# Meta rows of two projection pairs: fp32 products of four raw weight tiles in four 32-column tiles

## What is computed

```
meta = meta_tokens[None]                 # 16 rows
h = concatenate([meta, x1], axis=1)      # 16 + 512 rows, 2048 wide
hn = rmsnorm(h, attn_norm_w)
proj = hn @ w_in                         # a_k and a_v are columns 1024 to 3071
```

## Time and profile before

| | |
|---|---|
| median of three runs | 1591.24 us (1591.22 to 1592.08) |
| profiled execution | 1591.43 us, its span 1589.6 us |
| PE (matmul) | busy 99% of the span |
| DVE, ACT, POOL | 56%, 51%, 42% |
| granted TensorE clock, mean | 0.998 |

### The profile page before, as it was taken

How to read it: one execution, slowest core, us unless ns; L and a number is a source line. 1 busy time by engine, 2 the same in 40 slices (tenths; PEclk the granted TensorE clock), 3 DMA queues, 4 the chain that set the end, 5 groups by cost and what they waited for, 6 DMA issues and landing times.

```text
span 1589.6 us, 21772 instructions
## 1 busy us (share of the span) xinstructions
PE 1578.3 (99%) x8015; PEld 1301.0 (82%) x8015; DVE 887.9 (56%) x1843; ACT 812.2 (51%) x1692; POOL 674.9 (42%) x569
## 2 busy tenths in 40 slices
PE   9999999999999999999999999999999999999998
PEld 7788888888888888898787788888888888888886
DVE  4257657674357776468554441423355454876675
ACT  5456766764334455444344356444466664344561
POOL 5553434436766304675110035544444326664022
PEclk9999999999999999999999999999999999999999
DMA  9454655656888978858998847654554325625762
GB/s 346 127 177 97 155 125 158 160 119 144 195 204 187 240 242 264 233 177 187 258 254 284 210 155 273 191 140 140 160 156 128 102 79 140 152 80 152 245 239 106
DMA packets 139382, 285.39 MB, mean 180 GB/s; under 512 B 11227, under 2 KB 17820, under 8 KB 138604
## 3 DMA queue, kind: packets, MB, share of 16 engines
q1 hardware_dynamic: 85660, 164.49, 31.3%
q0 software_dynamic: 31664, 81.70, 25.1%
q10 hardware_dynamic: 21952, 37.81, 7.3%
HBM read 259.01 MB, written 92.06 MB: 221 GB/s over the span
## 4 chain that ended last, share of the span: by engine, by line
PE 98%; issue 1%; DVE 0%; ACT 0%; POOL 0%; DMA 0%; POOLq 0%; ACTq 0%; DVEq 0%
PE acc L718 15%; PE acc L720 15%; PE acc L719 15%; PE acc L734 4%; PE acc L736 4%; PE acc L735 4%; PE turn L1194 3%; PE acc L888 2%; PE acc L886 2%; PE acc L887 2%; PE sc L886 2%; PE sc L887 2%; PE turn L886 2%; PE turn L887 2%; PE sc L888 2%; PE turn L888 2%
## 5 line engine op out<-in xcount | busy, mean ns | idle before, releaser
L1939 POOL TENSOR_TENSOR w_lo<-w_raw,w_hi 128x512 fp32r<-128x512 f32 x341 | 509.5, 1503 | 654.3 <-ACT w_hi L1317 653.3
L1317 ACT ACTIVATE w_hi<-w_raw 128x512 fp32r<-128x512 f32 x565 | 354.2, 629 | 454.3 <-PE acc L720 182.4
L718 PE MATMUL acc<-w_hi,setA_hi 128*128 128x512 f32 (+1 forms) x820 | 330.5, 403 | 0.5 <-ACT stage L1331 0.4
L720 PE MATMUL acc<-w_hi,setA_lo 128*128 128x512 f32 (+1 forms) x820 | 315.8, 385 | 0.0
L719 PE MATMUL acc<-w_lo,setA_hi 128*128 128x512 f32 (+1 forms) x820 | 314.8, 384 | 0.0
L2364 DVE TENSOR_TENSOR w_lo<-w_raw,w_hi 128x512 fp32r<-128x512 f32 x224 | 154.6, 696 | 139.3 <-ACT w_hi L1317 138.7
L720 PEld LDWEIGHTS acc<-w_hi,setA_lo 128*128 128x128 f32 x820 | 153.9, 188 | 31.6
L718 PEld LDWEIGHTS acc<-w_hi,setA_hi 128*128 128x128 f32 x820 | 154.4, 188 | 26.2 <-issue 2.1
L719 PEld LDWEIGHTS acc<-w_lo,setA_hi 128*128 128x128 f32 x820 | 154.7, 189 | 24.0
L734 PE MATMUL acc<-setA_hi,w_hi 128*128 128x512 f32 x256 | 101.9, 398 | 0.0
L736 PE MATMUL acc<-setA_lo,w_hi 128*128 128x512 f32 x256 | 99.9, 390 | 0.0
(11 more groups left out here) (555 smaller groups left out, 3251.2 us busy)
## 6 DMA issues: line engine op xcount, KB each, us to landing
w_raw<-in_swa_w_in SPq DMA_DIRECT2D x35, 1024.0 KB, 7.3
w_raw<-in_w_in SPq DMA_DIRECT2D x32, 1024.0 KB, 5.2
w_raw<-sum_out SPq DMA_DIRECT2D x64, 256.0 KB, 4.6
sum_k<-in_w_in POOLq DMA_DIRECT2D x24, 512.0 KB, 6.5
sum_out<-in_swa_w_out POOLq DMA_DIRECT2D x24, 512.0 KB, 7.9
sum_v<-in_w_in POOLq DMA_DIRECT2D x24, 512.0 KB, 7.9
w_raw<-in_w_in SPq DMA_DIRECT2D x48, 256.0 KB, 5.5
sum_out<-in_w_out POOLq DMA_DIRECT2D x24, 512.0 KB, 6.5
```

Source lines behind the costliest of these rows:

```text
L718: mm(acc[t][:, 0:cols], hi[:, kc, rows], wh, start=(k == 0), stop=False)
L720: last = mm(acc[t][:, 0:cols], lo[:, kc, rows], wh, start=False, stop=(k == K - 1))
L1317: nc.scalar.activation(w_at(f)[0], raw_of(f), ACT.Copy).then_inc(done, 1)
L1939: nc.gpsimd.tensor_tensor(lo, raw_of(f), hi.bitcast(F32), ALU.subtract).then_inc(s_lo, 1)
```

## The change

The meta rows of the two pairs are no longer made from `w_hi` and `w_lo` but from `w_raw`, in plain fp32, with the meta tokens unsplit in a new tile `meta_full` (41 units of 16 columns: zeros, the tokens, their negatives). The stationary operand has 32 columns (16 rows for chunk a, 16 for chunk b), so that a product fills a quarter of the array's columns. Four pieces that belong to two successive values T of the pair's row index are taken together: piece n of the four writes partitions 32n to 32n+31 of `acc[2]`. The call `meta_products(c, M)`, M = 0 to 7, first waits for the landing of its four raw tiles, which are pieces 6M, 6M+1, 6M+3, 6M+4 in the first half (M < 4) and 6M, 6M+2, 6M+3, 6M+5 in the second. It stands after row block 0 of piece 1 for M = 0 and of piece 6M-1 for the others. `meta_product` and its 128 matmuls go; 16 calls of four fp32 matmuls come.

Since PE now reads `w_raw`, `free_tile` gains a second wait: the place of such a piece is free only when `s_used` shows that the piece at which `meta_products` stands has been done. The sum of four quarters instead of two parts takes DVE three additions instead of one; ACT's copy is as it was, of one quarter. The windows of `project_meta`, which stays, shrink from 96 to 80 columns. ACT fills `meta_full` with one activation more; DVE clears it once and makes two subtractions less.

```diff
-FULL = 96
+FULL = 80
@@ free_tile
                 eng.wait_ge(s_wlo, number[f - 8] + 1)
+            if f - 8 in meta_use:
+                eng.wait_ge(s_used, meta_use[f - 8])
@@
+        def meta_tiles(c, T):
+
+            if T < 8:
+                unit = SIGNED_AT + 3 * H1[c][T]
+                return (3 * T, unit + 1), (3 * T + 1, unit)
+            unit = 2 * (H2[c][T - 8] - 8)
+            return (3 * T, unit + 1), (3 * T + 2, unit)
+
+        meta_use = {}
+        for c in ("k", "v"):
+            for T in range(16):
+                for p, _ in meta_tiles(c, T):
+                    meta_use[B[c] + p] = B[c] + max(6 * (T // 2) - 1, 1) + 1 + 4
+
+        def meta_quarter(bank, n):
+
+            return bank[2 * META * n:2 * META * (n + 1)]
@@ PE
-            def meta_product(c, p, unit, start, stop):
-
-                wh, wl = w_at(B[c] + p)
-                mm(acc[2][0:FULL, :], meta_window(unit), wh, start=start, stop=False)
-                last = mm(acc[2][0:FULL, :], meta_window(unit), wl, start=False, stop=stop)
-                if stop:
+            def meta_products(c, M):
+
+                of = (*meta_tiles(c, 2 * M), *meta_tiles(c, 2 * M + 1))
+                for p, _ in of:
+                    slot, i, target = raw_at[B[c] + p]
+                    pe.wait_ge(s_tile[4 * slot + i], target)
+                for n, (p, unit) in enumerate(of):
+                    last = mm(meta_quarter(acc[2], n), meta_full[:, unit:unit + 2].rearrange("p a b -> p (a b)"),
+                              raw_of(B[c] + p), start=(M == 0), stop=(M == 7))
+                if M == 7:
                     last.then_inc(s_meta, 1)
@@ ACT
-                        nc.scalar.activation(metaT[:, SIGNED_AT + n:SIGNED_AT + 32:4], meta_f[:, 0:8], ACT.Copy, scale=sign)
+                        nc.scalar.activation(meta_full[:, SIGNED_AT + 1 + n:SIGNED_AT + 24:3], meta_f[:, 0:8], ACT.Copy, scale=sign)
+                    nc.scalar.activation(meta_full[:, 1:16:2], meta_f[:, 8:16], ACT.Copy)
@@ DVE
+                if m in (1, 2):
+                    for n in (0, 2):
+                        after(dve, V.tensor_tensor(total, meta_quarter(bank, n), total, ALU.add))
+                    V.tensor_tensor(total, meta_quarter(bank, 3), total, ALU.add).then_inc(s_mevac, 1)
+                    return
```

More of the change, by code:

```diff
@@ L70 @@
     SUM_SLOT[of] = slot
-SIGNED_AT, META_UNITS = 4 * KC + 1, 104
+SIGNED_AT, META_UNITS, FULL_UNITS = 16, 4 * KC + 2, 41
 HALF = S // 2
@@ L243, in build @@
         metaT = sb("metaT", [P, META_UNITS, META], F32R)
+        meta_full = sb("meta_full", [P, FULL_UNITS, META])
         alibi_h = over("alibi_h", [P, 2, ALIBI_AT[NT]], MASK)
@@ L1005, in project_mid @@
                                 product(c, p, i, setA_hi[:, h1[m], top], setA_lo[:, h1[m], top], X0[i], m == 0, m == 7)
[L1006 to L1011, removed]
                             elif j == 1:
@@ L1018, in project_mid @@
                                 product(c, p, i, mx_hi[:, 0, m, top], mx_lo[:, 0, m, top], acc[i][:], m == 0, m == 7)
-                                if i == 0:
-                                    meta_product(c, p, 4 * h1[m], False, False)
+                                if i == 0 and m == 0:
+                                    if c == "k":
+                                        pe.wait_ge(s_evac, 4 * E[14] + 4 + 3)
+                                    else:
+                                        pe.wait_ge(s_mevac, 3)
+                                    meta_products(c, 0)
                             else:
@@ L1026, in project_mid @@
                                 product(c, p, i, mx_hi[:, 1, m, top], mx_lo[:, 1, m, top], X1[i], m == 0, m == 7)
+                                if i == 0 and m % 2 == 1:
+                                    meta_products(c, m // 2 + 1)
                 for m in range(8):
@@ L1036, in project_mid @@
                                 product(c, p, i, setA_hi[:, h2[m], top], setA_lo[:, h2[m], top], X0[i], m == 0, m == 7)
-                                if i == 0:
-                                    meta_product(c, p, 4 * h2[m] + 1, False, False)
                             elif j == 1:
@@ L1046, in project_mid @@
                                 product(c, p, i, my_hi[:, 1, m, top], my_lo[:, 1, m, top], acc[i][:], m == 0, m == 7)
-                                if i == 0:
-                                    meta_product(c, p, 4 * h2[m], False, m == 7)
+                                if i == 0 and m in (1, 3, 5):
+                                    meta_products(c, m // 2 + 5)
                 for m in range(8):
@@ L2479, in _ @@
                         V.memset(metaT[:].bitcast(F32), 0.0)
+                        V.memset(meta_full[:], 0.0)
                 if m == 3:
@@ L2509, in _ @@
             dve.wait_ge(s_metaH, 1)
-            top_hi = metaT[:, 1:4 * 8:4].bitcast(F32)
-            V.tensor_tensor(metaT[:, SIGNED_AT + 2:SIGNED_AT + 32:4], meta_f[:, 0:8], top_hi, ALU.subtract)
-            V.tensor_tensor(metaT[:, SIGNED_AT + 3:SIGNED_AT + 32:4], top_hi, meta_f[:, 0:8], ALU.subtract)
             V.tensor_tensor(metaT[:, 3:4 * KC:4], meta_f[:], metaT[:, 1:4 * KC:4].bitcast(F32), ALU.subtract).then_inc(s_metaT, 1)
```

## The result

| | before | after |
|---|---|---|
| median of the runs | 1591.23 us (1590.13 to 1592.08) | 1603.34 us (1602.58 to 1604.01) |
| ratio | | 1.0075 (95% interval 1.0063 to 1.0087) |
| profiled execution, its span | 1591.43, 1589.6 us | 1604.01, 1602.2 us |
| up to the key pair's first product | 745.6 us | 747.8 us |
| key pair | 92.0 us | 103.6 us |

The kernel became 12.1 us slower; 5.9 us faster was predicted. The stages are read between starts of `product`'s first matmul on PE's timeline. In the profiled execution they differ by +2.2, +11.6, -2.1 and +0.9 us: nearly all of the loss is in the key pair. (Of the 2.2 us, 1.6 are waits of PE for POOL's low parts near 508 us in this one execution.

The account below looks back on a forecast made before the run. PE, busy 99% of the span, was taken to bound the kernel. Groups against removed matmuls gave -10.5 us, new waits +4.6, in sum -5.9: from 1591.43 to 1585.5 us, range 1580.2 to 1597.3.

Parts of the forecast that it names:

- The lower of the two bounds: On PE, the 16 new groups cost 19.7 us if four tiles run side by side; the other bound was 60.8.
- rows 5 and 6: Profile rows before, line 851 on PE: two fp32 column tiles start together and run fully side by side.
- The small edits: DVE's further sums, ACT's copy, meta_full's clearing and narrower project_meta windows: covered or too small to show, 0 us.
- Rival 1: In the pairs, loads are never late: -10.5 us, 1580.7 us; chance 0.08.
- The strict-order rival (4): On PE, matmuls start in strict order, a group takes five rounds, 2.5 us, 16 take 40.2: 1604 us; chance 0.06.
- Rival 3: On PE, moving operands can't be read for four tiles at once, a group costs 2.1 us: 1597.2 us; chance 0.14.
- the new waits: PE's waits for raw tiles needed earlier, in both pairs: 4.6 us, between nothing and 6.6.
- Landings of before against the time at which the group would stand: Late-tile estimate from the earlier trace: key pair M=2 and M=6, value pair M=5, 2.8 us in all.
- I cost it at nothing: SP's load of piece 6M+8, delayed about 3.5 us by free_tile's added wait: mostly covered before ACT wants it, 0 us.
- The bound of 6.6: Upper bound of PE's waiting: the key pair gives back all its gain, 5.3 us, and the value pair 1.3.
- Rival 2: Key pair bound by its loads, SP's later issues adding: over 7.3 us of stall, within 0.2% of before; chance 0.12.
- The sign that would show it wrong: PE's waits over 7 us or on low parts, or a group not near 1.2 us.

Follow-up runs that it names:

- experiment 1: Changed kernel, but its groups multiply resident token tiles instead of raw weight tiles, without landing waits or free_tile's added wait: 1579.86 us, ratio 0.9928.
- experiment 2: Changed kernel, its groups multiplying resident token tiles without landing waits, but with free_tile's added wait kept: 1579.32 us, ratio 0.9926.
- experiment 3: Changed kernel, its groups multiplying resident token tiles, with the landing waits kept but free_tile's added wait gone: 1590.34 us, ratio 0.9994.
- experiment 7: Changed kernel with groups M=1 to 7 one piece later (6M) and their places held as much longer: 1593.76 us, ratio 1.0025.
- experiment 8: Changed kernel with groups M=1 to 7 two pieces later (6M+1) and their places held as much longer: 1593.06 us, ratio 1.001.
- experiment 10: Changed kernel with groups M=1 to 7 one piece later (6M) and the first group one piece earlier (piece 0): 1594.12 us, ratio 1.0014.
- experiment 9: Changed kernel, but each pair's first group multiplies a resident token tile, with no landing wait or held places for it: 1597.74 us, ratio 1.0044.
- experiment 5: Changed kernel with most of POOL's block sums moved out of the pairs, one quarter staying at the key pair's start: 1598.51 us, ratio 1.0045.
- experiment 4: Changed kernel with 32 groups of two raw tiles instead of 16 of four, at piece 3T-1: 1599.45 us, ratio 1.0049.
- experiment 11: Change in the value pair alone; the key pair has the matmuls of the kernel before, on stand-in windows: 1592.51 us, ratio 1.001.
- experiment 12: Change in the value pair alone, its groups M=1 to 7 two pieces later; key pair with the earlier matmuls on stand-ins: 1589.39 us, ratio 0.9989.

## Why the prediction was wrong

**Right.** The groups alone are -11.3 us by experiment 1 (forecast -10.5), and a group costs 1.20 us (forecast 1.23). The lower of the two bounds, chosen by the form of rows 5 and 6, was the true one. The small edits cost nothing that experiments 1 and 2 would show. Rival 1 had the right worth for groups that never wait: 1580.7 against the 1579.86 of experiment 1.

The strict-order rival (4) gave 1604 us, within 1 us of what was measured, and that is a coincidence: it had 40.2 us for the groups and 2.8 of waits, where the traces have about 19 and 16.8. By mechanism it is out. The Trainium skill, "TensorE: Matmul & The Clock Gate", section on packing small matmuls, says that matmuls start in program order and that a weight load runs beside a matmul in flight only if the row groups differ. All tiles here are 128 rows deep, so their row groups are the same. Yet four start within 0.03 us, and a group of four costs as much as a group of two (1.20 and 1.18): the trace doesn't agree with the rule as it was applied to this case. Rival 3, the moving operands as a limit, is out by the same numbers.

**Wrong: the new waits.** The step that failed is the term "the new waits" of the sum: 4.6 us with an upper bound of 6.6. The trace has 16.8 us of waiting, and 4.7 us more that come of it. Three parts of the term failed.

1. "Landings of before against the time at which the group would stand" gave three late groups, and the trace of the need alone (experiment 3) has three, one at a place that was named for the key pair (M=2) and one for the value pair (M=5), 5.3 us in all. The kind was right, and so was the reading: the trace of before has these three and no others. But the landings were those of a single execution. In that same trace the last tile of three more groups lands only 0.2 to 0.5 us ahead of the need (M=5 and M=7 of the key pair, M=6 of the value pair). Ten executions give times over a range of 9 us, and their median puts the need at 10.5 us. The bound of 6.6 rested on that one execution too.

2. "I cost it at nothing", of SP's held loads. The reason given looked at when ACT wants piece 6M+8. Against that consumer it is right, and experiment 2 shows it: nothing. But the change brings a second, earlier consumer of the same loads, the group M+1, six pieces behind group M, and only four for M=0. The load that the hold delays and the tile that the next group wants early are the same: piece 10 is issued 4.8 us later and wanted 3.8 us after its issue, where the tiles that PE waits for in after take 5 to 8 us to land. Each edit was priced against the kernel before, none against the other. The square of experiments gives -0.5, +10.5 and, together, +23.5: the step that cost nothing is worth 13 us. In the traces of experiments 1 and 2 the hold takes the last tile's time from issue to need from 8.9 to 3.8 us at M=1 of the key pair and from 8.5 to 6.5 and 6.1 at M=2 and 3. In the second half that time is the same with and without it (6.0, 4.3, 5.9 and 6.0 against 5.9, 4.3, 5.7 and 6.0 us): there only the tiles ahead of the last go out later, and the late landings of M=5 and 7 in after aren't the last tile's later issue. What the hold adds there isn't separated from the early need. Moving the groups within the ring of eight places (experiments 7, 8 and 10) brings M=1 to five or six pieces behind the first group, but no group to more than six: it gains 9 to 10 us of the 23.5.

3. What a wait does to the clock wasn't in the sum. Against experiment 1 the key pair of after is 103.6 - 86.0 = 17.6 us longer: 12.9 are the waits, 4.7 the matmuls behind them. These are at the lower level of the clock, 1.2 GHz, after three of the five waits (4.5, 2.2 and 2.5 us), 1.5 to 1.6 us each time by the excess of the distances over those of experiment 1; after the two others (2.1 and 1.5) PE goes on at 2.4 GHz. The value pair has no such place, and 90.3 - 86.4 = 3.9 us is its waits exactly.

With that the sum closes to about 1 us for each trace: the 1579.9 of experiment 1, plus the waits, plus the excess behind them, plus the later (or less the earlier) start of the key pair.

| | waits | excess | start | sum | measured |
|---|---|---|---|---|---|
| after | 16.8 | 4.7 | +1.9 | 1603.3 | 1604.0 |
| experiment 3 | 5.3 | 1.6 | -0.3 | 1586.5 | 1587.6 |
| experiment 8 | 10.2 | 3.2 | 0.0 | 1593.3 | 1593.7 |
| experiment 9 | 13.9 | 6.0 | -0.9 | 1598.9 | 1599.5 |
| experiment 10 | 11.3 | 6.0 | -0.8 | 1596.4 | 1597.1 |

**Rival 2** named the stall from SP's later issues, with 0.12. Two things about it were off. It put the time within 0.2% of before, and nothing in the trace limited the stall to that. And it saw the cause in the DMA engines' share of 0.98. The share isn't what limits: experiment 1 runs 6 us faster at 0.98, and the change is slower at 0.86. It is latency: in after the last tile of a group lands 4 to 8 us after its issue (single loads up to 10.7), and 4 to 7 us lie between issue and need. The traffic matters as far as it lengthens landings, which experiment 5 shows for all waits but key M=1, where it took none away.

**The sign that would show it wrong** was put down rightly: "if PE's waits come to over 7 us".

Open: why one and the same load (piece 16 of the key pair) lands after 4.1 us in after and after 10.0 in experiment 2 isn't settled. That this is what makes the runs scatter is likely, but each version has a single trace. Whether the change would pay with twelve places of `w_raw` instead of eight was not tried.

## What to carry to other kernels

A step that releases a buffer later and one that needs the next transfer earlier may each be free and still cost much together: take the ring as one loop, and count from the release to the next need against the longest landing, for the new consumers too. A load that never made anyone wait shows nothing of how late it may come, so its landing in one trace bounds nothing; before PE is made to wait on it, give it the longest landing in the stretch (10.4 us in the trace before), or batch fewer tiles. A gain of 0.7 us per group (four pairs of 0.47 against 1.2) is lost by a single microsecond of waiting, and a wait of 2 us or more can cost another 1.6 us behind it.

## What the runs showed of the hardware

Column tiles: four fp32 matmuls of 32 columns, 128 rows deep and 512 columns long, run side by side. At the full clock the two rounds start 0.43 to 0.47 us apart, and the group costs 1.20 us with the way in and out; two tiles cost 1.18 (experiment 4).

The clock: in the traces of the change and of experiments 3, 5 and 7 to 12 the matmuls went on at 1.2 GHz behind every group that had waited 2.2 us or more (16 of them), and behind none that had waited 1.7 us or less. Around 2 us there are both: the clock fell after waits of 1.98 and 2.12 us, not after 2.04, 2.10 and 2.11. (These are waits by the distances; the idle time in the view is 0.07 us less.) Two groups of the key pair of after show how near the cases lie, the first at M=3 after 2.14 us of idle time, the second at M=5 after 2.04:

```profile
783.67 1.07 PE L1011 MATMUL acc<-w_raw,meta_full 128*32 128x512 f32 x8 [2.14 <-DMA w_raw<-sum_k]
784.67 0.57 PE L907 MATMUL sc<-w_hi,mx_hi 128*128 128x512 f32 x1
785.03 0.63 PE L908 MATMUL sc<-w_lo,mx_hi 128*128 128x512 f32 x1
785.46 0.63 PE L909 MATMUL sc<-w_hi,mx_lo 128*128 128x512 f32 x1
...
806.12 1.07 PE L1011 MATMUL acc<-w_raw,meta_full 128*32 128x512 f32 x8 [2.04 <-DMA w_raw<-in_w_in]
807.12 0.50 PE L907 MATMUL acc<-w_hi,my_hi 128*128 128x512 f32 x1
807.46 0.39 PE L908 MATMUL acc<-w_lo,my_hi 128*128 128x512 f32 x1
807.68 0.40 PE L909 MATMUL acc<-w_hi,my_lo 128*128 128x512 f32 x1
```

In the first the group itself is at full rate, and the distances behind it are 0.36 and then 0.43 us; in the second they are 0.34 and then 0.22. At M=1 and M=7 the fall had come before the group's end. Fourteen of the 18 falls cost 1.5 to 1.6 us each, the other four, behind waits of 3.0 to 5.1 us, 2.0 to 2.8 us.
